# The last residual of a two-block decoder kernel: adding on VectorE, or by transfers that accumulate onto the output

## What is computed

```python
def first_block(...):
    h = concatenate([meta, x], axis=1)
    n = rmsnorm(h, g_pre_mix)
    z = n @ w_in
    mix = concatenate([short_conv_group(z...), rwkv7_group(z...)], axis=-1) @ w_out
    h = h + rmsnorm(mix, g_post_mix)
    f = conv_glu(rmsnorm(h, g_pre_ffn), w_gate_up, conv_ffn, w_down)
    h = h + rmsnorm(f, g_post_ffn)
    return h[:, N_META:]

def second_block(x, ...):
    h = rms_norm(x, norm_g[i, 0])
    m = swa_sink_attention(h, ...)
    x = x + rms_norm(m, norm_g[i, 1])
    h = rms_norm(x, norm_g[i, 2])
    x = x + rms_norm(conv_ffn(h, ffn_w_up[i], ffn_conv[i], ffn_w_down[i]), norm_g[i, 3])
    return x
```

## Time and profile before

| | us |
|---|---|
| median of 3 runs | 2339.54 |
| lowest, highest | 2339.06, 2340.32 |
| span of the profiled execution | 2337.8 |
| median less span | 1.7 |
| TensorE busy | 2317.6 (99%) |
| VectorE busy | 1529.9 (65%) |
| ScalarE busy | 1071.4 (46%) |
| GpSimd busy | 123.3 (5%) |

### The profile page before, as it was taken

The page is one execution under the profiler, slowest core; times in us unless marked ns, Lnnn a source line. Parts: engine busy times, 40 slices in busy tenths (PEclk is TensorE's granted clock), DMA queues, the critical chain, the costliest instruction groups (busy, mean ns, idle before and its releaser), DMA issues.

```text
span 2337.8 us, 52157 instructions
## 1 busy us (share of the span) xinstructions
PE 2317.6 (99%) x20796; PEld 2170.5 (93%) x20796; DVE 1529.9 (65%) x1965; ACT 1071.4 (46%) x1371; POOL 123.3 (5%) x156
## 2 busy tenths in 40 slices
PE   9999999999999999999999999999999999999997
PEld 9999999999999999998889999899888888888897
DVE  5678877748766665654444867648877877774444
ACT  5543344455444434343444555655444444444442
POOL 2000000013000000000000300012000000000000
PEclk9999999999999999999999999999999999999999
DMA  7553333355555555555555473354655555555553
GB/s 251 173 161 121 115 107 128 137 183 171 189 180 179 183 185 180 181 186 187 188 186 187 155 243 127 123 193 155 196 189 191 178 190 194 181 193 188 187 186 120
DMA packets 117103, 406.03 MB, mean 174 GB/s; under 512 B 12864, under 2 KB 20000, under 8 KB 116704
## 3 DMA queue, kind: packets, MB, share of 16 engines
q1 hardware_dynamic: 112080, 396.07, 52.1%
q10 hardware_dynamic: 4880, 7.82, 1.0%
HBM read 401.69 MB, written 2.15 MB: 173 GB/s over the span
## 4 chain that ended last, share of the span: by engine, by line
PE 93%; DVE 5%; issue 1%; ACT 1%; DMA 0%; DVEq 0%; ACTq 0%
PE ps L1765 24%; PE ps L1767 12%; PE ps L1769 12%; PE ps L1771 11%; PE ps L1770 11%; PE ps L1740 2%; PE ps L1742 2%; PE ps L1741 2%; PE ps L1954 2%; PE ps L1944 2%; PE ps L1945 2%; PE ps L1946 2%; PE ps L2310 1%; PE ps L2312 1%; PE ps L2311 1%; DVE wl L977 1%
## 5 line engine op out<-in xcount | busy, mean ns | idle before, releaser
L977 DVE TENSOR_TENSOR wl<-raw,wh 128x1024 fp32r<-128x1024 f32 x743 | 909.4, 1236 | 674.0 <-ACT wh L558 673.7
L558 ACT ACTIVATE wh<-raw 128x1024 fp32r<-128x1024 f32 x743 | 776.3, 1056 | 896.1 <-PE ps L1767 361.7
L1769 PE MATMUL ps<-xh,wh 128*128 128x256 f32 (+2 forms) x2048 | 582.2, 284 | 1.6 <-DVE xl L1010 0.9
L1771 PE MATMUL ps<-xh,wl 128*128 128x256 f32 (+2 forms) x2048 | 580.5, 283 | 0.0
L1770 PE MATMUL ps<-xl,wh 128*128 128x256 f32 (+2 forms) x2048 | 580.1, 283 | 0.0
L1765 PE MATMUL ps<-x,wh 128*128 128x512 f32 x1280 | 448.2, 393 | 0.8 <-DVE wl L977 0.8
L1769 PEld LDWEIGHTS ps<-xh,wh 128*128 128x128 f32 x2048 | 387.0, 189 | 3.6 <-DVE wl L977 1.9
L1770 PEld LDWEIGHTS ps<-xl,wh 128*128 128x128 f32 x2048 | 387.2, 189 | 0.2
L1771 PEld LDWEIGHTS ps<-xh,wl 128*128 128x128 f32 x2048 | 386.7, 189 | 0.0
L1765 PE MATMUL ps<-act,wh 128*128 128x512 f32 x1056 | 369.7, 393 | 0.0
L1767 PE MATMUL ps<-x,wl 128*128 128x256 f32 x1280 | 357.1, 279 | 0.0
(11 more groups left out here) (306 smaller groups left out, 3117.7 us busy)
## 6 DMA issues: line engine op xcount, KB each, us to landing
raw<-in_gate_up SPq DMA_DIRECT2D x176, 512.0 KB, 3.8
raw<-in_down SPq DMA_DIRECT2D x176, 512.0 KB, 4.3
raw<-in_up SPq DMA_DIRECT2D x176, 512.0 KB, 4.2
raw<-in_w_in SPq DMA_DIRECT2D x103, 512.0 KB, 3.8
raw<-in_in SPq DMA_DIRECT2D x48, 512.0 KB, 3.9
raw<-in_w_out SPq DMA_DIRECT2D x32, 512.0 KB, 4.4
raw<-in_out SPq DMA_DIRECT2D x32, 512.0 KB, 3.7
bias<-bias_rows ACTq DMA_DIRECT2D x1, 4096.0 KB, 25.5
```

What stands on the lines that cost most here:

```text
L558: act.activation(wh[:, slot], raw[:, slot], ACT.Copy).then_inc(high_ready, 1)
L977: dve.tensor_tensor(wl[:, slot], raw[:, slot], wh[:, slot].bitcast(F32), ALU.subtract).then_inc(low_ready, 1)
L1769: pe.matmul(out, w_high, hi, start=(k == 0), stop=False)
L1771: last = pe.matmul(out, w_low, hi, start=False, stop=(k == 2 * per - 1))
```

## The change

VectorE keeps the multiplies, in four parts of four tiles, and drops the adds. SyncE stores all of h to `out` ahead of the loads of down2's weights. GpSimd waits for that store and then, for each multiplied part, issues a transfer from mixf to the same place of `out` that adds (`accum_op=ALU.add`): what stands there is read, the part is added to it, and the sum is written.

```diff
@@ names of semaphores
+        h_stored, scaled = sem("h_stored"), sem("scaled")
+        LAST_PARTS = [(0, 4), (4, 4), (8, 4), (12, 4)]
@@ SyncE, in the loop over the projections
                 first = FIRST[name]
+                if name == "down2":
+                    sp.wait_ge(h_ready, 16 * 3)
+                    sp.dma_start(d["out"], h[:, :, TU:L]).then_inc(h_stored, 16)
@@ SyncE, after the loop
-            for k, tiles in ((0, 4), (4, 4), (8, 4), (12, 2), (14, 2)):
-                sp.wait_ge(h_ready, 16 * 3 + k + tiles)
-                sp.dma_start(d["out"][:, k:k + tiles, :], h[:, k:k + tiles, TU:L]).then_inc(stored, 16)
-            sp.wait_ge(stored, 16 * 5)
+            sp.wait_ge(stored, 16 * len(LAST_PARTS))
@@ GpSimd, at its end
+            pool.wait_ge(h_stored, 16)
+            for x, (k, count) in enumerate(LAST_PARTS):
+                pool.wait_ge(scaled, x + 1)
+                pool.dma_start(d["out"][:, k:k + count, :], mixf[:, k:k + count, :], accum_op=ALU.add).then_inc(stored, 16)
@@ VectorE, at its end
-            for k, count in ((0, 4), (4, 4), (8, 4), (12, 2), (14, 2)):
-                residual(mixf, SEQ, TU, k, count, ps[:, 3, 0:SEQ])
+            for k, count in LAST_PARTS:
+                tiles = mixf[:, k:k + count, :]
+                dve.tensor_tensor(tiles, tiles, over(ps[:, 3, 0:SEQ], count), ALU.mult).then_inc(scaled, 1)
```

## The result

The changed kernel takes **2346.82 us** (median of 8 runs, 2345.68 to 2348.0) against 2339.89 for the kernel before in the same comparison (8 runs, 2339.06 to 2341.57). The ratio is 1.0029, with a 95% interval of 1.0020 to 1.0038: 6.9 us slower, where no change was forecast and slower had a chance of 0.23.

What follows compares the result with a forecast made beforehand. TensorE paces all but the end, a VectorE chain and one store. First multiply done 2326.2 + 2.0 fixed + 4 x 2.3 transfers + 0.4 end = 2337.8, plus 1.7 around the span: 2339.5 us, range 2335.5 to 2348.

Steps and rivals of the forecast that it cites:

- the tail: From the first of the last multiplies to the end of the span: VectorE's chain, one store, and the end.
- VectorE's share: Last multiplies: five adds removed, four multiplies of 1.22 us each left, VectorE done 5.6 us earlier; nearly certain.
- SyncE's share: Five issues and landings removed at the end; early 2 MB store ahead of down2's loads, costed at nothing.
- GpSimd's share: Four adding transfers of 512 KB added at the end, 2.0 us fixed and 2.3 us of the engines each.
- fixed part: Time of a transfer besides its occupation of the engines: 2.0 us, including 0.9 for GpSimd's issue.
- issues spaced wider than the multiplies: Sign in the profile after, at GpSimd's four transfers: GpSimd itself is the bound, and the fixed part is wrong.
- Rival C: Adding packets in the DMA engines each pay a round trip; X = 8, time 2362.3, decides over 3.5; chance 0.20.
- X: Occupation of the DMA engines by one adding transfer of 512 KB: taken as 2.3 us, forecast 1.9 to 2.7.

## Why the prediction was wrong

Where it stood: the tail was to stay at 12.8 us; it is 20.2. Of the 7.4 us between, the profile with room for 76 descriptors puts 20.2 - 15.6 = 4.6 on the gap and what came with it (4.2 by the medians, each against its own before), and 15.6 - 12.8 = 2.8 on the transfers themselves (2.7 by the medians). The measured 2346.82 lies inside the range that was given, up to 2348, but by luck: that end stood for adding transfers that occupy the engines for up to 4.4 us each, and they don't.

- **VectorE's share held.** Four multiplies in 4.62 us, against 4.64 worked out.
- **SyncE's share held.** The early store is hidden. It landed 9.8 us after its issue at 2055.18, so at 2065.0 and 1.4 later than I had it. down2's first load landed at 2066.3, and ScalarE turned to that chunk at 2068.3: 2.0 us of slack were left.
- **GpSimd's share failed, in its fixed part.** The step was: its queue is free, so four issues go out behind the multiplies, and 2.0 us stand ahead of the engines' time once. The queue was free, but an issue needs room for its descriptors, and the fourth had none: it waited 9.4 us, until all three ahead of it had landed. The kernel was built with 1024 bytes for them, a constant in the unchanged part of the code that no row of before could show, as nothing was issued by GpSimd. The text named "issues spaced wider than the multiplies" as what would prove the fixed part wrong, but had neither mechanism nor price for it, nor a rival that ends slower for this reason. Rival C, which carried most of the slower side, was another one and is not what happened: in the kernel with 76 descriptors X is 2.5, far below its 3.5, and a packet takes 0.33 us, not 0.44.
- **The rest of the fixed part was too small.** From the first multiply's end to the first landing I had 2.0 + 2.3 = 4.3. With 76 descriptors it is 2328.70 - 2328.06 = 0.6 to the start of the issue and 5.8 to the landing, 6.4 in all: 2.1 more. The issue itself was right (0.9 taken, 0.86 to 1.16 measured). The plain transfer lands in 3.1, so of the adding one's 5.8 the longer occupation explains 2.5 - 1.4 = 1.1, and some 1.6 us more belong to the first transfer alone. The packets show where: its first one starts 1.6 us after the issue against 1.3, and from there to its last one it takes 3.9 us, where a later transfer adds 2.5. Its early packets take up to 1.6 us, against 0.33 later on. Why they do stays open; I had taken this part from plain stores.
- **X was nearly right.** 2.3 taken, 2.5 measured without the gap, inside the forecast's own 1.9 to 2.7. In the changed kernel the landings of the first three are 3.9 and 2.5 apart; the second was late there, and it adds up to 1.2 us to the tail by the third landing (12.0 against 10.8 us after the first issue). One of its packets, begun at 2332.06, took 2.05 us, so single DMA engines fell behind; why, I can't tell. Plain transfers land 1.4 apart (the first 3.1, the last 7.4 us after the first issue).
- **The sum with these sizes:** first multiply 1.22, then 6.4 to the first landing, 3 x 2.5, 0.5 to the end: 15.6, as measured. With the gap: the third landing at 1.22 + 0.64 + 11.99 = 13.85, 0.26 to the fourth issue, 5.65 to its landing, 0.44 to the end: 20.2, as measured.

So the mechanism of the forecast (VectorE's gain is given back by transfers in a row) was right and comes to 2.8 us slower, not to nothing; and a second mechanism, unforeseen, made it 6.9.

The change itself buys little to set against this. Taking 5.6 us off VectorE was worth 12.8 - 9.7 = 3.1 us in the kernel whose transfers are plain, which leaves the addition out. The addition in the transfers then costs 15.6 - 9.7 = 5.9 us even with room for all descriptors.

## What to carry to other kernels

A transfer that adds onto DRAM also reads what stands there: for 512 KB cost 5.8 us to the first landing where a plain one has 3.1, and 2.5 us for each one behind it where a plain one has 1.4. Against an add on an engine it can win only where it is off the end of the chain; no run here tries that. Before issuing DMAs from GpSimd, count what their descriptors need against the room reserved for them: one transfer too many doesn't wait for a slot but for everything under way. Here, if all the reserved bytes can be used, an adding transfer of 128 rows needs 273 to 304 of them and a plain one 129 to 170. And a store that shares the engines with adding transfers lands behind them, so mixing the two at the end gives back most or all of what was taken off the compute engine. An add shared between VectorE and GpSimd is no way out either: with both operands in SBUF the two take turns.

## What the runs showed of the hardware that I had not expected

- GpSimd resumes issuing only when all its transfers have landed: 0.3 us after the third with 1024 and with 1088 bytes, 0.3 after the second with 768, 0.35 after the third with 512 and plain.
- Four adding transfers of 128 rows don't fit in 1088 reserved bytes per partition and do in 1216; four plain ones fit in 1024 and not in 512.
- An adding transfer of 512 KB with none ahead of it lands 5.5 to 5.9 us after its issue in each profile, the fourth of the changed kernel too (5.7), against 2.9 to 3.2 for a plain one.
- The first issue begins 0.6 us after the multiply it waits for has ended; SyncE's first issue, at 2327.6, follows its add's end, 2327.53, in 0.1 or less.
- VectorE's adds of SBUF by SBUF and GpSimd's take turns: each is held until about the end of the other's that began first (VectorE 1.91 for 1.23, and 2.50 for three tiles; GpSimd 2.25 for 1.27).
